# First-block attention: bias sum, negation and maximum in one VectorE instruction, the query's gate sum added by TensorE

## The chip, the cores and the metric

The kernel runs on one core of a Trainium2 chip. The metric is the device time of one launch in microseconds (us). A core has TensorE (PE in the profile; its weight loads are PEld), VectorE (DVE), ScalarE (ACT), GpSimd (POOL) and SyncE (SP, which here issues the weight loads from memory).

## The reference, cut to what matters

Two model blocks run one after the other. Only the attention of the first block is touched. It is run twice (DEPTH = 2 layers), each time with 8 heads of width 64 on 256 tokens, in query blocks of 128:

```python
cum = jnp.cumsum(log_f.astype(jnp.float32), axis=1).transpose(0, 2, 1)   # 8 x 256
...
logits = jnp.einsum("bhqd,bhkd->bhqk", qi, k).astype(jnp.float32) * scale
logits = logits + ci[..., :, None] - cum[:, :, None, :]
logits = jnp.where(kpos[None, :] <= qpos[:, None], logits, -jnp.inf)
p = jax.nn.softmax(logits, axis=-1)
return jnp.einsum("bhqk,bhkd->bhqd", p.astype(v.dtype), v)
```

So each logit is a product of query and key, plus the gate sum of the query (`ci`), minus the gate sum of the key, masked. The rest of the first block (a 31-tap convolution, a gated recurrence, an output projection, a large product-key layer) and the whole second block stay as they are.

## The kernel before, in words

Every engine has one program in a fixed order; semaphores order them against each other. Weights come as tiles of 128x1024 into a ring of four, are split by ACT into a high part `Wh` (L1207) and by DVE into a low part `Wl` (L1698), and PE multiplies both. A layer of the first block begins with 20 such tiles of input projection (16 tiles `m_` = 0..15 and 4 value tiles), then comes the attention, then the output projection.

Within the projection, PE also does small work between tiles. At `m_ == 12` it turns the gate sums `cum` (8 partitions x 256) into columns in bank 5, and DVE copies them to `cT` (L1890). In `gate_spread` PE spreads the negated key sums `ncum` over all 128 partitions with the selector `sel` (8x128 for a head), and DVE adds the mask in `gate_bias` and keeps the result in `biasT` (L1875 to L1877). The attention begins when the last `gate_bias` is done.

The attention is a software pipeline over `h` = 0..9. PE's turn `h` holds, in this order:

- the scores of head h+1 (`head_scores`): one fp32 matmul of 128 columns for the first query block, and one of 256 for the second, into bank 4 or 5. The operands lie on partitions 0 to 63 for an even head and 64 to 127 for an odd one;
- in turns 0 and 1, 4 and 5 filler matmuls (`keep_clock`, bf16, 512 columns, result unused);
- the product of probabilities and values of head h-2 (from the transposed `PT`);
- three transposes of the probabilities `Pm` of head h-1 (L749), which wait for DVE's `p_ready`;
- in turns 2 to 6, 3 filler matmuls.

DVE's turn `h` holds: two `scalar_tensor_tensor` for head h (scores + `cT` + `biasT`, 128 and 256 columns, L1927 and L1929), a wait for its own semaphore `att_sc`, two `tensor_reduce` for the negated maximum (L1933, L1934), then for head h-1 the reciprocal of the sums (L1939), two scalings of `Pm` (L1940, L1941, which signal `p_ready`), and two taps of the convolution (four instructions of L1856).

ACT's turn holds the two exponentials with their sums (L1319, L1321), the copy of the transposed probabilities (L1328), and now and then a copy of a finished head pair (L1333) and of a part of the mixer's output (L1310, in turn 6). The buffers of scores, `Pm` and `PT` are double.

After turn 9 come a layer norm and 18 filler matmuls, and the output projection.

Of the kernel before, what the change touches and what calls it, by code (L numbers as in the profile page):

```python
# [12 lines left out]
ALU = mybir.AluOpType  # L13
ACT = mybir.ActivationFunctionType
AXX = mybir.AxisListType.X


P = 128
D = 1024
C = D // P  # L20
T = 256
T2 = 2 * T
L = 2
HEADS, HD = 8, 64
# [249 lines left out]
def build(nc, wts, mod_d, cst_d, keys_d, mla_d, bias_d, x_d, ctx_d, out_d, stop_after=None):  # L274
    ctx = ExitStack()
    with ctx:
# [85 lines left out]
        PT = [arena[:, i * 3 * P:(i + 1) * 3 * P] for i in range(2)]  # L362
        cT = area(2, HEADS)

# [178 lines left out]
        def _(pe):  # L543
# [120 lines left out]
            def gate_spread(l, i):  # L664

                if i:
                    pe.wait_ge(S("bc_ev"), 5 * l + i)
                for h in (2 * i, 2 * i + 1):
                    m = mm(bank[6 - i % 2][:, (h % 2) * T:(h % 2 + 1) * T], sel[0:HEADS, h, :], ncum[0:HEADS, :], True, True)
                m.then_inc(S("bc_mm"), 1)  # L670
# [6 lines left out]
            for l in range(L):  # L677
# [4 lines left out]
                for m_ in range(16):  # L682
# [21 lines left out]
                    if m_ == 12:  # L704
                        pe.wait_ge(S("cum_ready"), l + 1)
                        pe.wait_ge(S("rg_ev"), 2 * l + 2)
                        for tt in range(2):
                            m = mm(bank[5][:, tt * HEADS:(tt + 1) * HEADS], cum[0:HEADS, tt * P:(tt + 1) * P],
                                   ident[0:HEADS, 0:HEADS], True, True)
                        m.then_inc(S("bc_mm"), 1)  # L710
                    if m_ in (13, 14):
# [6 lines left out]
                pe.wait_ge(S("proj_ev"), N_EV * (l + 1))  # L718
                pe.wait_ge(S("bc_ev"), 5 * (l + 1))
                def head_scores(h):  # L720
                    po, hc, b = slice(64 * (h % 2), 64 * (h % 2) + 64), h // 2, bank[4 + h % 2]
                    if h >= 2:
                        pe.wait_ge(S("att_sc"), HEADS * l + h - 1)
                    mm(b[:, 0:P], qT[po, hc, 0:P], kT[po, hc, 0:P], True, True)
                    mm(b[:, P:3 * P], qT[po, hc, P:T], kT[po, hc, :], True, True).then_inc(S("att_mm"), 1)

                head_scores(0)
                for h in range(HEADS + 2):
# [22 lines left out]
                    if 2 <= h < 7:  # L751
                        keep_clock(3, bank[3])
                    if h == HEADS:
# [425 lines left out]
        def _(act):  # L1179
# [67 lines left out]
            for l in range(L):  # L1247
# [64 lines left out]
                for h in range(HEADS + 2):  # L1312
                    if h < HEADS:
                        act.wait_ge(S("att_mx"), HEADS * l + h + 1)
                        if h >= 2:
                            act.wait_ge(S("pt_mm"), HEADS * l + h - 1)
                        nm = col[:, 8 + 2 * (h % 2):10 + 2 * (h % 2)]
                        sm = col[:, 12 + 2 * (h % 2):14 + 2 * (h % 2)]
                        nc.scalar.activation(Pm[h % 2][:, 0:P], sc[h % 2][:, 0:P], ACT.Exp, bias=nm[:, 0:1],  # L1319
                                             accum_out=sm[:, 0:1])  # L1320
                        nc.scalar.activation(Pm[h % 2][:, P:], sc[h % 2][:, P:], ACT.Exp, bias=nm[:, 1:2],  # L1321
                                             accum_out=sm[:, 1:2]).then_inc(S("att_exp"), 1)
# [324 lines left out]
        def _(dve):  # L1647
# [158 lines left out]
            for l in range(L):  # L1806
# [62 lines left out]
                def gate_bias(i):  # L1869

                    dve.wait_ge(S("bc_mm"), 5 * l + i + 2)
                    src = bank[6 - i % 2][:, :].rearrange("p (a b) -> p a b", a=2)
# [15 lines left out]
                seq(v.tensor_tensor(bx[:, :, :], ig[:, :, :], xr[:, :, :], ALU.mult))  # L1888
                dve.wait_ge(S("bc_mm"), 5 * l + 1)
                v.tensor_copy(cT[:, :, :], bank[5][:, 0:2 * HEADS].rearrange("p (a b) -> p a b", a=2)).then_inc(S("bc_ev"), 1)  # L1890
                taps(14, 16)
# [20 lines left out]
                gate_bias(3)  # L1912
                dve.wait_ge(S("bc_ev"), 5 * (l + 1))
                def mix_low(p):
# [6 lines left out]
                for h in range(HEADS + 1):  # L1921
                    if h < HEADS:
                        dve.wait_ge(S("att_mm"), HEADS * l + h + 1)
                        if h >= 2:
                            dve.wait_ge(S("att_exp"), HEADS * l + h - 1)
                        s_, b = sc[h % 2], bank[4 + h % 2]
                        v.scalar_tensor_tensor(out=s_[:, 0:P], in0=b[:, 0:P], scalar=cT[:, 0, h:h + 1],  # L1927
                                               in1=biasT[:, h, 0:P], op0=ALU.add, op1=ALU.add)
                        v.scalar_tensor_tensor(out=s_[:, P:], in0=b[:, P:3 * P], scalar=cT[:, 1, h:h + 1],  # L1929
                                               in1=biasT[:, h, P:], op0=ALU.add, op1=ALU.add).then_inc(S("att_sc"), 1)  # L1930
                        dve.wait_ge(S("att_sc"), HEADS * l + h + 1)
                        nm = col[:, 8 + 2 * (h % 2):10 + 2 * (h % 2)]
                        v.tensor_reduce(nm[:, 0:1], s_[:, 0:P], AXX, ALU.max, negate=True)  # L1933
                        v.tensor_reduce(nm[:, 1:2], s_[:, P:], AXX, ALU.max, negate=True).then_inc(S("att_mx"), 1)  # L1934
                    if h >= 1:
# [519 lines left out]
```

## Time and profile before

| | |
|---|---|
| median of 3 runs | 3141.77 us (3140.1 to 3142.35) |
| the profiled execution's own time | 3144.92 us |
| its span (first to last instruction) | 3143.0 us |
| PE busy, share of the span | 97% |
| DVE busy | 72% |
| ACT busy | 44% |
| mean granted TensorE clock | 0.992 |
| attention with its prologue and layer norm | about 40 us, twice (98 to 138 us and 1098 to 1138 us) |

The profile is of one execution; its own time lies 3.15 us above the median of the timed runs, and 1.9 us of it lie outside the span. Busy shares are means over stages that have different limits, so the attention is read from its own stretch. Times of single instructions are start and duration on one engine; an engine may begin an instruction before the record of the one ahead of it has ended, so the distance from one start to the next is what an instruction costs.

### The profile page before, as it was taken

Reading aid. Unit: us, or ns where it says so; the run is one execution under the profiler, and the core shown is the slowest. Engines: PE = TensorE matmul, PEld = TensorE weight load, DVE = VectorE, ACT = ScalarE, POOL = GpSimd, SP = SyncE. Lnnn points to the kernel's source line nnn. Section 1 sums busy time; section 2 is a strip of 40 time slices with the busy share of each in tenths; the row PEclk is TensorE's granted clock in tenths of the full one; section 3 lists DMA queues with packets and bytes.
Section 4 is the critical chain, followed back from the end, with each engine's and each line's share of the span. In section 5 each row is a group of like instructions: output and inputs, shape, how many; then the busy total and the mean of one; then the engine's idle time right before and its main releaser. Section 6 shows DMA issues by size and latency. Waiting matters only on the chain. (4 is left out here: it accounts for less than half of the span.)

```text
span 3143.0 us, 59178 instructions
## 1 busy us (share of the span) xinstructions
PE 3049.7 (97%) x22446; PEld 2667.8 (85%) x22446; DVE 2270.8 (72%) x3842; ACT 1377.4 (44%) x2167; POOL 248.0 (8%) x195
## 2 busy tenths in 40 slices
PE   8899999999999989999999999999999989998999
PEld 7699988989887769998998988776778878874999
DVE  7778877787887869887777798676456764665446
ACT  5445444443444544535344344445432223436444
POOL 0064000000000017100000000000001100001000
PEclk9999999999999999999999999999999999999999
DMA  4245565464555324646556456420035542321354
GB/s 166 87 141 196 167 208 192 164 246 151 168 187 190 131 72 162 209 160 233 170 189 216 156 167 220 137 98 8 15 116 191 201 161 94 107 88 61 128 182 155
DMA packets 131892, 478.44 MB, mean 152 GB/s; under 512 B 14593, under 2 KB 16641, under 8 KB 131329
## 3 DMA queue, kind: packets, MB, share of 16 engines
q1 hardware_dynamic: 115904, 416.72, 39.6%
q0 software_dynamic: 15808, 59.25, 5.7%
q8 instruction: 122, 2.00, 0.3%
q14 instruction: 58, 0.47, 0.1%
HBM read 474.87 MB, written 1.05 MB: 151 GB/s over the span
## 5 line engine op out<-in xcount | busy, mean ns | idle before, releaser
L1698 DVE TENSOR_TENSOR Wl<-ring,Wh 128x1024 fp32r<-128x1024 f32 x720 | 878.4, 1222 | 560.9 <-ACT Wh L1207 558.6
L545 PE MATMUL bank<-HR,Wh 128*128 128x256 f32 (+1 forms) x7488 | 1143.0, 303 | 6.6 <-DVE HR L1918 4.0
L1207 ACT CAST Wh<-ring 128x1024 fp32r<-128x1024 f32 x788 | 824.1, 1046 | 609.0 <-PE bank L545 609.0
L545 PEld LDWEIGHTS bank<-HR,Wh 128*128 128x128 f32 x7488 | 1011.8, 191 | 65.7 <-issue 14.1
L545 PE MATMUL bank<-HR,Wl 128*128 128x256 f32 (+1 forms) x3744 | 612.0, 300 | 10.1 <-DVE Wl L1698 10.1
L545 PE MATMUL bank<-Wh,HR 128*128 128x512 f32 x2304 | 577.2, 394 | 1.1 <-DVE HR L2105 0.8
L545 PEld LDWEIGHTS bank<-HR,Wl 128*128 128x128 f32 x3744 | 525.3, 191 | 33.9 <-DVE Wl L1698 11.5
L545 PEld LDWEIGHTS bank<-Wh,HR 128*128 128x128 f32 x2304 | 428.5, 188 | 96.0 <-issue 8.4
L545 PE MATMUL bank<-arena 128*128 128x32 f16 (+5 forms) x5128 | 305.1, 213 | 15.4 <-DVE arena L1877 6.2
L545 PE MATMUL bank<-Wl,HR 128*128 128x512 f32 x1152 | 306.1, 389 | 0.0
L1436 ACT ACTIVATE arena<-bank 128x256 f32 (+1 forms) x256 | 98.3, 384 | 470.5 <-PE bank L545 470.3
L545 PEld LDWEIGHTS bank<-arena 128*128 128x128 f16 (+3 forms) x5128 | 223.7, 112 | 84.7 <-issue 41.7
L545 PEld LDWEIGHTS bank<-Wl,HR 128*128 128x128 f32 x1152 | 216.3, 188 | 45.3
L2400 POOL TENSOR_TENSOR Wl<-ring,Wh 128x1024 fp32r<-128x1024 f32 x68 | 163.8, 2416 | 101.3 <-ACT Wh L1207 101.0
L2081 DVE TENSOR_TENSOR arena<-arena 128x2048 f16<-128x2048 f16 x128 | 155.8, 1218 | 0.1
L2409 POOL DMA_DIRECT2D HA<-mods x48 | 36.0, 749 | 1361.1 <-DVE arena L1672 1024.0
L545 PE MATMUL bank<-FR,Wh 128*128 128x512 f32 (+1 forms) x704 | 132.0, 340 | 8.1 <-DVE modv L1681 8.1
L545 PEld LDWEIGHTS bank<-FR,Wh 128*128 128x128 f32 x704 | 110.6, 192 | 23.0 <-DVE modv L1681 8.5
L1674 DVE SCALAR_TENSOR_TENSOR arena<-arena,csil 128x1024 f32<-128x1024 f32 x84 | 104.1, 1280 | 6.9 <-DMA arena<-mods 4.8
L2105 DVE TENSOR_TENSOR HR<-arena,HR 128x256 fp32r<-128x256 f32 x256 | 106.7, 420 | 1.1 <-ACT HR L1380 0.9
L1674 DVE SCALAR_TENSOR_TENSOR arena<-HA,csil,arena 128x1024 f32<-128x1024 f32 x84 | 107.1, 1316 | 0.0
L2089 DVE TENSOR_TENSOR arena<-arena 128x512 f16<-128x512 f16 x256 | 97.3, 421 | 12.2
(254 smaller groups left out, 2153.9 us busy)
## 6 DMA issues: line engine op xcount, KB each, us to landing
ring<-weights SPq DMA_DIRECT2D x788, 512.0 KB, 3.3
HA<-mods POOLq DMA_DIRECT2D x48, 512.0 KB, 4.0
arena<-mods POOLq DMA_DIRECT2D x48, 512.0 KB, 3.6
arena<-bias POOLq DMA_DIRECT2D x16, 256.0 KB, 3.2
arena<-keys POOLq DMA_DIRECT2D x2, 1024.0 KB, 5.3
arena<-mla POOLq DMA_DIRECT2D x1, 1536.0 KB, 6.4
X<-x SPq DMA_DIRECT2D x1, 1024.0 KB, 6.6
X<-context POOLq DMA_DIRECT2D x1, 1024.0 KB, 7.1
```

The costliest lines, as they stand in the source:

```text
L545: return nc.tensor.matmul(out, lhsT, rhs, start=first, stop=last)
L1207: nc.scalar.copy(Wh[:, i % SPL], ring[:, i % RAW]).then_inc(S("hi_done"), 1)
L1436: nc.scalar.activation(o, bank[s % 2][:, 0:T], ACT.Gelu_apprx_tanh).then_inc(S("h_ev"), 1)
L1674: m = v.scalar_tensor_tensor(out=out[:, j], in0=w, scalar=by, in1=out[:, j], op0=ALU.mult, op1=ALU.add)
L1698: v.tensor_tensor(Wl[:, i % SPL], ring[:, i % RAW], Wh[:, i % SPL], ALU.subtract).then_inc(S("lo_done"), 1)
L2081: v.tensor_tensor(Aoh[s % 2], pairs(if12h[:, 0, at]).broadcast_to([P, BT // 2, P, 2]), iotar.unsqueeze(1).broadcast_to([P, BT // 2, P, 2]) ...
L2089: m = v.tensor_tensor(Bg[s % 2][:, part], Boh[s % 2], pairs(gpart[:, part, at]).broadcast_to([P, BT // 2, EQ, 2]), ALU.mult)
L2105: v.tensor_tensor(Hl[:, s % MV, 0:T], GH[q % 2][:, bass.ds(it * R + s, 1), :] .rearrange("p o t -> p (o t)"), Hh[:, s % MV, 0:T], ALU.subt ...
L2400: nc.gpsimd.tensor_tensor(Wl[:, i % SPL], ring[:, i % RAW], Wh[:, i % SPL], ALU.subtract)\
L2409: pool.dma_start(mod_slot(n), mod_d[n].rearrange("p (a b) -> p a b", a=4)).then_inc(S(f"mod_in{n % 2}"), 16)
```

## The change

Four edits, all for the attention of the first block.

- The query's gate sum is no longer turned into `cT` and added by DVE. PE adds it in the scores' bank, with a matmul of `cum` (8 partitions x 128, the stationary operand) and the head's selector (8x128), once for each 128 columns: three more fp32 matmuls for a head. The step at `m_ == 12`, DVE's copy and one semaphore count go.
- DVE's four instructions for a head become two `tensor_tensor_reduce`: each writes -(scores + `biasT`) and its minimum, which is the negated maximum of the logits.
- ACT's exponentials take scale -1.0.
- PE's filler matmuls in turns 2 to 6 go from 3 to 1, and the scores of head h+1 wait for `att_mx` instead of `att_sc`.

```diff
@@ gate_spread
-                if i:
-                    pe.wait_ge(S("bc_ev"), 5 * l + i)
+                if i >= 2:
+                    pe.wait_ge(S("bc_ev"), 4 * l + i - 1)
@@ PE, m_ == 12
                         pe.wait_ge(S("rg_ev"), 2 * l + 2)
-                        for tt in range(2):
-                            m = mm(bank[5][:, tt * HEADS:(tt + 1) * HEADS], cum[0:HEADS, tt * P:(tt + 1) * P],
-                                   ident[0:HEADS, 0:HEADS], True, True)
-                        m.then_inc(S("bc_mm"), 1)
@@ PE, head_scores
                     if h >= 2:
-                        pe.wait_ge(S("att_sc"), HEADS * l + h - 1)
-                    mm(b[:, 0:P], qT[po, hc, 0:P], kT[po, hc, 0:P], True, True)
-                    mm(b[:, P:3 * P], qT[po, hc, P:T], kT[po, hc, :], True, True).then_inc(S("att_mm"), 1)
+                        pe.wait_ge(S("att_mx"), HEADS * l + h - 1)
+                    mm(b[:, 0:P], qT[po, hc, 0:P], kT[po, hc, 0:P], True, False)
+                    mm(b[:, 0:P], cum[0:HEADS, 0:P], sel[0:HEADS, h, :], False, True)
+                    mm(b[:, P:3 * P], qT[po, hc, P:T], kT[po, hc, :], True, False)
+                    for a in range(2):
+                        m = mm(b[:, (1 + a) * P:(2 + a) * P], cum[0:HEADS, P:T], sel[0:HEADS, h, :], False, a == 1)
+                    m.then_inc(S("att_mm"), 1)
@@ PE, turns 2 to 6
-                        keep_clock(3, bank[3])
+                        keep_clock(1, bank[3])
@@ ACT
-                        nc.scalar.activation(Pm[h % 2][:, 0:P], sc[h % 2][:, 0:P], ACT.Exp, bias=nm[:, 0:1],
+                        nc.scalar.activation(Pm[h % 2][:, 0:P], sc[h % 2][:, 0:P], ACT.Exp, bias=nm[:, 0:1], scale=-1.0,
@@ DVE, projection
-                dve.wait_ge(S("bc_mm"), 5 * l + 1)
-                v.tensor_copy(cT[:, :, :], bank[5][:, 0:2 * HEADS].rearrange("p (a b) -> p a b", a=2)).then_inc(S("bc_ev"), 1)
@@ DVE, attention
-                        v.scalar_tensor_tensor(out=s_[:, 0:P], in0=b[:, 0:P], scalar=cT[:, 0, h:h + 1],
-                                               in1=biasT[:, h, 0:P], op0=ALU.add, op1=ALU.add)
-                        v.scalar_tensor_tensor(out=s_[:, P:], in0=b[:, P:3 * P], scalar=cT[:, 1, h:h + 1],
-                                               in1=biasT[:, h, P:], op0=ALU.add, op1=ALU.add).then_inc(S("att_sc"), 1)
-                        dve.wait_ge(S("att_sc"), HEADS * l + h + 1)
                         nm = col[:, 8 + 2 * (h % 2):10 + 2 * (h % 2)]
-                        v.tensor_reduce(nm[:, 0:1], s_[:, 0:P], AXX, ALU.max, negate=True)
-                        v.tensor_reduce(nm[:, 1:2], s_[:, P:], AXX, ALU.max, negate=True).then_inc(S("att_mx"), 1)
+                        v.tensor_tensor_reduce(s_[:, 0:P], b[:, 0:P], biasT[:, h, 0:P], -1.0, 3.0e38, ALU.add, ALU.min, nm[:, 0:1])
+                        v.tensor_tensor_reduce(s_[:, P:], b[:, P:3 * P], biasT[:, h, P:], -1.0, 3.0e38, ALU.add, ALU.min,
+                                               nm[:, 1:2]).then_inc(S("att_mx"), 1)
```

## Rows read from the trace of the kernel before

**Rows 1.** The page, part 1: busy us of each engine, share, instructions.

```profile
PE 3049.7 (97%) x22446; PEld 2667.8 (85%) x22446; DVE 2270.8 (72%) x3842; ACT 1377.4 (44%) x2167; POOL 248.0 (8%) x195
```

**Rows 2.** Windows, attention's turns: length, PE, PEld, DVE, ACT, POOL busy, clock, DMA.

```profile
103.50:125.00 21.50, 15.76 (x79) 8.78 (x80) 21.08 (x67) 10.13 (x35) 0.00 (x0) 1.00 0.00 1
```

**Rows 3.** Timeline, one turn of the pipeline: start, us, engine, line, instruction, idle before.

```profile
108.53 0.34 DVE L1927 SCALAR_TENSOR_TENSOR arena<-bank,arena 128x128 f32<-128x128 f32 x1
108.79 0.47 DVE L1929 SCALAR_TENSOR_TENSOR arena<-bank,arena 128x256 f32<-128x256 f32 x1
...
109.83 0.15 DVE L1939 RECIPROCAL col<-col 128x2 f32<-128x2 f32 x1
...
110.62 0.55 PE L749 MATMUL bank<-K,arena 128*128 128x128 f32 x3 [0.70 <-DVE arena L1941]
...
112.07 0.34 DVE L1927 SCALAR_TENSOR_TENSOR arena<-bank,arena 128x128 f32<-128x128 f32 x1
```

**Rows 4.** Timeline of PE, the same turn, narrow windows (rows*columns of the array).

```profile
107.08 0.55 PE L749 MATMUL bank<-K,arena 128*128 128x128 f32 x3 [1.35 <-DVE arena L1941]
107.47 0.81 PE L545 MATMUL bank<-K 128*128 128x512 bf16 x3
107.90 0.38 PE L545 MATMUL bank<-K 128*128 128x512 bf16 x1
108.21 0.37 PE L545 MATMUL bank<-arena 64*128 64x128 f32 x1
108.42 0.49 PE L545 MATMUL bank<-arena 64*128 64x128 f32 x2
108.75 0.38 PE L545 MATMUL bank<-arena 64*128 64x256 f32 x1
109.06 0.43 PE L545 MATMUL bank<-arena 128*64 128x256 f32 x1
```

**Rows 5.** Timeline of PE, a key spread (8 rows) and the value tile behind it.

```profile
87.08 0.48 PE L545 MATMUL bank<-arena 8*128 8x256 f32 x1
87.40 0.38 PE L545 MATMUL bank<-arena 8*128 8x256 f32 x1
...
88.13 0.50 PE L545 MATMUL bank<-Wh,HR 128*128 128x512 f32 x1
```

**Rows 6.** Timeline of PE, the attention's start: scores of heads 0 and 1, fillers, first transposes.

```profile
99.15 0.39 PE L545 MATMUL bank<-arena 64*128 64x128 f32 x2 [3.12 <-DVE arena L1877]
...
100.01 1.04 PE L545 MATMUL bank<-K 128*128 128x512 bf16 x4
...
103.54 0.55 PE L749 MATMUL bank<-K,arena 128*128 128x128 f32 x3 [0.46 <-DVE arena L1941]
```

**Rows 7.** Timeline of DVE, two tensor_tensor_reduce in a row in the second block.

```profile
2842.80 0.69 DVE L2332 CUSTOM_DVE_ANT_0 arena<-bank,arena 128x512 f32<-128x512 f32 x1 [0.17 <-PE bank L545]
...
2843.42 0.69 DVE L2332 CUSTOM_DVE_ANT_0 arena<-bank,arena 128x512 f32<-128x512 f32 x1
```

**Rows 8.** Timeline, the last turns: transposes of heads 5 and 7, ACT's work between them.

```profile
121.23 0.55 PE L749 MATMUL bank<-K,arena 128*128 128x128 f32 x3 [0.70 <-DVE arena L1941]
...
121.82 0.48 ACT L1328 COPY arena<-bank 128x384 f32<-128x384 f32 x1 [0.28 <-PE bank L749]
122.19 0.62 ACT L1310 CAST HR<-arena 128x512 fp32r<-128x512 f32 x1
...
124.09 0.40 ACT L1319 ACTIVATE arena<-arena,col 128x128 f32<-128x128 f32 x1 [1.28 <-DVE col L1934]
...
124.89 0.19 ACT L1321 ACTIVATION_READ_ACCUMULATOR arena<-arena,col 128x1 f32 x1
...
127.05 0.55 PE L749 MATMUL bank<-K,arena 128*128 128x128 f32 x3 [0.30 <-DVE arena L1941]
```

**Rows 9.** Timeline of PE, the step at `m_ == 12` and the tile behind it.

```profile
69.77 0.61 PE L545 MATMUL bank<-K,arena 8*128 8x8 f32 x4
...
70.31 2.18 PE L545 MATMUL bank<-HR,Wh 128*128 128x256 f32 x16
```

More of the change, by code:

```diff
@@ L362, in build @@
         PT = [arena[:, i * 3 * P:(i + 1) * 3 * P] for i in range(2)]
-        cT = area(2, HEADS)
         top[0] = 16384
@@ L718, in _ @@
                 pe.wait_ge(S("proj_ev"), N_EV * (l + 1))
-                pe.wait_ge(S("bc_ev"), 5 * (l + 1))
+                pe.wait_ge(S("bc_ev"), 4 * (l + 1))
                 def head_scores(h):
@@ L1318, in _ @@
                         sm = col[:, 12 + 2 * (h % 2):14 + 2 * (h % 2)]
-                        nc.scalar.activation(Pm[h % 2][:, 0:P], sc[h % 2][:, 0:P], ACT.Exp, bias=nm[:, 0:1],
+                        nc.scalar.activation(Pm[h % 2][:, 0:P], sc[h % 2][:, 0:P], ACT.Exp, bias=nm[:, 0:1], scale=-1.0,
                                              accum_out=sm[:, 0:1])
-                        nc.scalar.activation(Pm[h % 2][:, P:], sc[h % 2][:, P:], ACT.Exp, bias=nm[:, 1:2],
+                        nc.scalar.activation(Pm[h % 2][:, P:], sc[h % 2][:, P:], ACT.Exp, bias=nm[:, 1:2], scale=-1.0,
                                              accum_out=sm[:, 1:2]).then_inc(S("att_exp"), 1)
@@ L1869, in gate_bias @@
                 def gate_bias(i):
-                    dve.wait_ge(S("bc_mm"), 5 * l + i + 2)
+                    dve.wait_ge(S("bc_mm"), 4 * l + i + 1)
                     src = bank[6 - i % 2][:, :].rearrange("p (a b) -> p a b", a=2)
@@ L1912, in _ @@
                 gate_bias(3)
-                dve.wait_ge(S("bc_ev"), 5 * (l + 1))
+                dve.wait_ge(S("bc_ev"), 4 * (l + 1))
                 def mix_low(p):
```

## The prediction

> **What bounds the kernel now.** I read the page first. PE is busy 97% of the span [rows 1], but that is a mean over stages, so it says nothing yet of the attention. The windows of the attention's turns say more: of 21.5 us DVE is busy 21.08, PE 15.76, ACT 10.13, and no weights move [rows 2]. DVE sets the pace there. The timeline shows how. From one L1927 to the next is 3.54 us (108.53 to 112.07), with no idle time on DVE, and PE's transposes wait 0.70 us for DVE's L1941 [rows 3]. So in a turn PE has some slack, but not much, and the change takes work from DVE and gives work to PE. The question is which of the two is longer afterwards.
>
> **What PE's passes cost.** An fp32 matmul is two records. In the score part the first pass of 128 columns starts at 108.21, the second at 108.42, the third (256 columns) 0.11 later and the fourth at 108.75; before them the last filler starts at 107.90 and the fillers are 0.22 apart (107.47 to 107.90 is two of them) [rows 4]. So a pass of 128 columns takes 0.11, one of 256 takes 0.22, a filler 0.22. Two places don't fit. The filler at 107.90 is through at 108.11, but the scores start at 108.21; and the second pass comes 0.21 behind the first and not 0.11. That is 0.09 plus 0.10 lost where the array goes from 128 rows to 64. The same two losses stand where it goes from 64*128 to 128*64 (108.75 + 0.22 = 108.97, next start 109.06), and from 128 rows to 8 and back: the first 8-row pass has 0.32 to the second, where 0.22 is the stream, and from 87.40 three passes of 0.22 end at 88.05, while the next tile starts at 88.13 [rows 5]. I take 0.19 for a change of the array's shape into an fp32 matmul.
>
> **DVE, part by part.** Removed are the four instructions from 108.53 to 109.83, 1.30 us a head, a wait on DVE's own semaphore included [rows 3]. Added are two `tensor_tensor_reduce`. The second block has this instruction at 512 columns, 0.61 from start to start with its accumulator read hidden [rows 7]. 0.53 of it is the stream at one column in 1.04 ns (its cost over 128-column and 256-column neighbours of the same kind grows like that: L1927 and L1929 differ by 0.13 in duration for 128 columns), the rest is fixed, 0.08. So 0.21 and 0.35, together 0.56. DVE's turn would be 3.54 - 1.30 + 0.56 = 2.80 us. Even at the 0.61 of the 512-column form twice it would be 3.46. ACT's exponentials with scale -1 cost what they did. If DVE alone counted, seven turns would give 5 us a layer.
>
> **PE, part by part.** A turn now: transposes to fillers 0.39 (107.08 to 107.47), three fillers and the change to 64 rows 0.74, scores 0.85 (108.21 to 109.06), values 0.70 (0.27, 0.22, 0.11, 0.11) and 0.09 to the next transposes; sum 2.77 against 3.54, a slack of 0.77 [rows 4]. The change takes two fillers out, -0.43. It adds three fp32 matmuls of 128 columns, six passes, 0.65. And it alternates 64-row and 8-row matmuls: 64, 8, 64, 8, 8, then the values. That is three more changes of shape in each head. No row shows a change between 64 and 8 rows. From below it costs nothing (heads 0 and 1, on different halves of the rows, start together at 99.15 and lose nothing [rows 6]); from above I put the gap plus a full pass of latency, 0.09 + 0.27, as if each change waited for the record's end. Nearest are the changes above, all 0.19, whichever two shapes meet, so I take 0.19, three times 0.57. PE's turn becomes 2.77 - 0.43 + 0.65 + 0.57 = 3.56. PE then sets the pace, at what DVE had: the turn gains nothing.
>
> The Trainium skill, in TensorEngine Tiling (Array Packing), section Key Properties, says that changing the tiling mode, not just the tile, drains TensorE. The page speaks against this change, since 64 and 8 rows are two modes; by it the sum is mine, and without it the sum is that of the first rival.
>
> **The start.** Today the scores of heads 0 and 1 run together, 99.15 to 100.01, 0.86 [rows 6]. With 8-row matmuls between they can't: a head's scores are 0.85 + 0.65 + 0.57 = 2.07, two are 4.1, so the fillers start 3.2 later. Head 2's scores are another 1.2 longer. The first transposes, which today wait 0.46 for DVE at 103.54 [rows 6], came then at 99.15 + 4.11 (two heads) + 0.97 (4 fillers, change) + 2.07 (head 2) + 1.09 (5 fillers) = 107.4, which is 3.9 late. DVE's part of that (first maximum, exponential, reciprocal, scaling) is done before 105. From there to the transposes of head 5 are five turns, the first without filler and so 0.2 shorter: 17.6 instead of 17.7. They start 3.7 later than 121.23.
>
> **The end.** The last two turns have no scores. Today 5.82 us pass from the transposes of head 5 to those of head 7 (121.23 to 127.05), because DVE is late [rows 8]. After the change DVE is ahead and the chain is ACT's: copy and mixer copy done 1.6 after the transposes (121.23 to 122.81), head 7's exponentials 1.0 (124.09 to 125.08), copy of head 6 about 0.45, values 0.8: 3.8. That gives back 2.0. So a layer's attention ends 3.7 - 2.0 = 1.7 later.
>
> **The projection.** The four 8x8 passes go: 69.77 to 70.31, 0.54 [rows 9]. PE has no other wait there, the low part for the next tile is ready only about 0.1 before it would be needed, and the attention's start follows PE through the last value tile. I take 0.5 a layer; from below nothing. DVE's copy of 0.17 is hidden beside PE.
>
> **Sum.** (1.7 - 0.5) x 2 = +2.4 us. Span 3143.0 becomes 3145.4, with 1.9 outside it 3147.3 for a profiled execution; the median stood 3.15 lower than the profiled one, so 3144.2. What follows the attention (layer norm, 18 fillers, output projection) only moves. The clock was 1.00 in the turns [rows 2]; PE is now busier there, so two fillers less shouldn't lower it.
>
> A change under 0.2%, 6.3 us, can't be told from none here.
>
> **Rivals.**
>
> *Changes between 64 and 8 rows are free.* For it: heads 0 and 1 lose nothing between two 64-row halves. Against: those have one shape, and every change of shape in the rows costs. Then PE's turn is 2.99, still over DVE's 2.80; the first transposes come 2.2 late, head 5's 0.8 early, the end 2.8 early, with the projection 3.3 a layer: 6.6, time 3135.2, just past the bound. If only the 0.09 is lost each time it lies halfway to the forecast, near 3140.
>
> *Odd heads overlap.* Odd heads lie on rows 64 to 127, the 8-row operands on rows 0 to 7, and two matmuls on different rows did run together [rows 6]. Then, changes being free too, an odd head's scores stay at 0.85 and PE averages 2.7 a turn, just under DVE's 2.80: head 5's transposes come 3.4 early, the end 5.4, with the projection 5.9 a layer, time 3130. Against: the shapes differ, and both write one bank.
> The Trainium skill's page TensorE: Matmul & The Clock Gate, Part 3, says that matmuls on different row groups overlap; the trace agrees for two 64-row ones (starts both at 99.15), and by that rule the time would be this rival's.
>
> *A change from 64 to 8 rows costs more than the others* and the kernel is slower. Its place is the same three changes, since both sides add into one bank, one on top of the other's sum. At 0.36 each a head's scores are 0.5 longer, eight of them before head 5's transposes make 4.1 us a layer: 3152. It decides from 0.27 a change on: the bound is 3.15 a layer, 1.2 are in the sum, and 1.95 over 24 changes is 0.08 more than 0.19.
>
> *DVE's instruction doesn't get cheaper.* If it took twice its stream, DVE's turn would be 3.3, still under PE's 3.56: no effect on the time.
>
> **How the numbers follow.** The forecast (PE's turn about as long as DVE's was) 0.60, its own range 3141 to 3147.5 (0.05 either way in each of nine turns). Changes free 0.11, half of them 0.10, overlap 0.08, dearer changes 0.10, other 0.01. Faster by over 0.2%: the overlap 0.08, most of the free case 0.08, a little of the rest 0.02, together 0.18. Slower: the dearer case 0.10 and 0.01. Within: 0.71. The predicted time is 3144.2. The range reaches from just past the free case, 3134, to 3149, leaving out the overlap and most of the dearer case.
>
> **What would show it.** In the trace after: the 128-column scores followed by an 8-row pass 0.2 later than the stream; a head's scores 2.07 from first to last; transposes 3.5 to 3.6 apart and no longer released by DVE but following PE; DVE idle 0.7 a turn; `tensor_tensor_reduce` 0.21 and 0.35 apart; transposes of head 0 near 107, of head 7 near 128. A turn of 3.0 says the changes are free, one of 2.8 released by DVE that they overlap, one over 3.8 that they are dear.

## The result and the profile after

The changed kernel takes 3159.28 us (median of 4 runs, 3155.96 to 3167.41), beside 3142.06 for the kernel before (4 runs, 3140.1 to 3143.82): a ratio of 1.0057, interval 1.0045 to 1.0068, some 17 us slower. The forecast was 3144.2 with a range to 3149. The profiled execution took 3157.23 us, with a span of 3155.4 and a mean granted clock of 0.988. The other three runs show how much hangs on that last number: 3155.96 at 0.988, 3161.34 at 0.987, 3167.41 at 0.985. The two profiled executions are only 12.3 us apart (3144.92 and 3157.23), the medians 17.2. What is taken from the traces below explains the 12; the other 5 lie in the choice of the profiled runs, and no trace shows where.

Part 1 of the page of the changed kernel answers to [rows 1]:

```profile
PE 3074.2 (97%) x22514; PEld 2683.2 (85%) x22514; DVE 2260.7 (72%) x3840; ACT 1377.1 (44%) x2167; POOL 248.3 (8%) x195
```

PE has 68 records more and 24.5 us more of busy time. At full clock the change would be 14 of these: 16 heads by 1.22 (0.65 of passes and 0.57 of changes), less 20 fillers of 0.22 and two steps of 0.54. So the other matmuls must have become longer somewhere. The page doesn't say where: its clock line, in 40 slices, is 9 everywhere. Windows do. Of the changed kernel: the low stretch of layer 0's attention and the rest of its turns, then 40 us around each attention, then the low stretch of layer 1 (each row: length, busy times of PE, PEld, DVE, ACT and POOL, clock, DMA share, GB/s):

```profile
99.60:113.30 13.70, 13.70 (x39) 7.60 (x38) 6.34 (x26) 2.58 (x10) 0.00 (x0) 0.50 0.00 1
113.30:130.10 16.80, 16.80 (x86) 10.53 (x85) 12.11 (x49) 6.74 (x26) 0.00 (x0) 1.00 0.01 1
95.00:135.00 40.00, 36.11 (x150) 21.79 (x150) 23.44 (x87) 14.28 (x46) 0.00 (x0) 0.83 0.05 16
1095.00:1135.00 40.00, 36.88 (x142) 22.16 (x140) 22.44 (x78) 12.93 (x37) 0.00 (x0) 0.79 0.14 48
1103.10:1120.20 17.10, 16.39 (x44) 9.41 (x44) 6.91 (x28) 2.38 (x10) 0.00 (x0) 0.50 0.10 31
```

The same windows of the kernel before:

```profile
95.00:135.00 40.00, 29.15 (x145) 15.64 (x145) 32.07 (x92) 21.05 (x55) 0.00 (x0) 1.00 0.06 25
1095.00:1135.00 40.00, 29.14 (x145) 15.63 (x145) 32.07 (x92) 21.04 (x55) 0.00 (x0) 1.00 0.07 25
```

The clock column is the result. Before, it was 1.00 in both attentions (2.4 GHz); now it is 0.50 (1.2 GHz) for 13.7 us in the first and 17.1 us in the second, and 1.00 again from 113.3 and 1120.2 on. Look at PE's busy time in the low stretch of layer 0: 13.70 of 13.70. Nothing is idle there; the engine is full of work and slow. The two falls don't come at the same place: in layer 0 at 99.6, within the first scores, in layer 1 at 1103.1, in the 3.12 us of idle time and 0.7 before the first scores.

Timeline of PE in the changed kernel, layer 0, to be laid beside [rows 4, 6]:

```profile
97.97 6.25 PE L544 MATMUL bank<-arena 64*128 64x128 f32 x20 [3.12 <-DVE arena L1876]
104.15 1.89 PE L544 MATMUL bank<-K 128*128 128x512 bf16 x4
105.97 3.81 PE L544 MATMUL bank<-arena 64*128 64x128 f32 x10
109.71 2.31 PE L544 MATMUL bank<-K 128*128 128x512 bf16 x5
111.81 0.85 PE L748 MATMUL bank<-K,arena 128*128 128x128 f32 x3
...
119.35 0.55 PE L748 MATMUL bank<-K,arena 128*128 128x128 f32 x3
119.73 0.38 PE L544 MATMUL bank<-K 128*128 128x512 bf16 x1
120.04 2.96 PE L544 MATMUL bank<-arena 64*128 64x128 f32 x14
122.93 0.55 PE L748 MATMUL bank<-K,arena 128*128 128x128 f32 x3
...
133.91 0.55 PE L748 MATMUL bank<-K,arena 128*128 128x128 f32 x3
```

The ten passes of head 2's scores take 3.81 at 1.2 GHz, and two heads 6.18 (97.97 to 104.15), the first 1.6 of it at full clock. Once the clock is back, the turn is regular: 119.35 to 122.93 is 3.58. The transposes at the front of the turn have no release in brackets any more: they follow PE itself. DVE waits instead. Timeline of PE and DVE in one such turn, narrow windows, beside [rows 3, 4]:

```profile
116.46 0.49 PE L544 MATMUL bank<-arena 64*128 64x128 f32 x2
116.88 0.37 PE L544 MATMUL bank<-arena 8*128 8x128 f32 x1
117.29 0.48 PE L544 MATMUL bank<-arena 64*128 64x256 f32 x1
117.91 0.37 PE L544 MATMUL bank<-arena 8*128 8x128 f32 x1
118.55 0.43 PE L544 MATMUL bank<-arena 128*64 128x256 f32 x1
```

```profile
118.66 0.29 DVE L1925 CUSTOM_DVE_ANT_0 arena<-bank,arena 128x128 f32<-128x128 f32 x1 [0.69 <-PE bank L544]
118.87 0.42 DVE L1926 CUSTOM_DVE_ANT_0 arena<-bank,arena 128x256 f32<-128x256 f32 x1
119.22 0.16 DVE L1932 RECIPROCAL col<-col 128x2 f32<-128x2 f32 x1
```

These are the scores of head 4, an even one. They take 2.09 (116.46 to 118.55). The next turn, with head 5, is as long (119.35 to 122.93). DVE's two instructions are 0.21 and 0.35 apart, and it stands idle 0.69 for PE in every turn.

**Where the time went.** From the first scores to the last transposes of layer 0 it is now 35.94 us (97.97 to 133.91), where it was 27.90 [rows 6, 8]: 8.0 longer. A turn is 3.58 at full clock and 6.47 at half clock (a_fill_idle, below), so each microsecond at half clock loses 1 - 3.58/6.47 = 0.447; 13.7 lose 6.1. The rest, 1.9, is what the forecast had as 1.7. The same two ends in layer 1:

```profile
1103.81 7.51 PE L544 MATMUL bank<-arena 64*128 64x128 f32 x20 [3.12 <-DVE arena L1876]
...
1140.92 0.55 PE L748 MATMUL bank<-K,arena 128*128 128x128 f32 x3
```

That is 37.11, 9.2 longer. Of the low stretch 16.4 us lie behind the first scores; they lose 16.4 x 0.447 = 7.3, and the rest is 1.9 again. The start of layer 0's attention came 1.18 earlier, half of it from the step taken out at `m_ == 12`; the other half was there before the first tile of the projection, so the change has no part in it. So the clock costs 6.1 + 7.3 = 13.4 us in the two attentions, and the instructions of the change 1.9 + 1.9, less 0.6 twice for the projection, 2.6: together 16.0. The span grew by 12.4. The difference of 3.6 is the lead of 0.6 and 3.0 from behind the attentions. The kernel before had 3.4 us at 0.50 there, as its windows show, and the changed one has none: the same stretch of the output projection on PE takes 8.93 before (138.39 to 147.32) and 7.42 after (145.26 to 152.68), 1.5 less in each layer. That the low stretch of before isn't there any more is luck: no edit aims at it.

```profile
138.40:141.80 3.40, 3.40 (x16) 3.40 (x17) 0.00 (x0) 0.44 (x1) 0.69 (x1) 0.50 0.37 77
1138.50:1141.90 3.40, 3.40 (x17) 3.40 (x18) 0.00 (x0) 0.63 (x1) 0.55 (x1) 0.50 0.52 159
```

### The profile page after: what moved, and what is told of

The parts are those of the page before. It is cut to its first block and busy times, and to the rows that moved or that the text cites. A ratio compares the mean times of both kernels' runs of the same rounds, so it can differ in the third digit from the quotient of the medians.

```text
span 3155.4 us, 59312 instructions
## 1 busy us (share of the span) xinstructions
PE 3074.2 (97%) x22514; PEld 2683.2 (85%) x22514; DVE 2260.7 (72%) x3840; ACT 1377.1 (44%) x2167; POOL 248.3 (8%) x195
## 5 line engine op out<-in xcount | busy, mean ns | idle before, releaser
L544 PE MATMUL bank<-arena 128*128 128x32 f16 (+8 forms) x5224 | 335.5, 217 | 16.1 <-DVE arena L1876 6.2
L544 PEld LDWEIGHTS bank<-arena 128*128 128x128 f16 (+4 forms) x5224 | 244.4, 115 | 95.9 <-issue 50.4
L2393 POOL TENSOR_TENSOR Wl<-ring,Wh 128x1024 fp32r<-128x1024 f32 x68 | 163.9, 2418 | 98.2 <-ACT Wh L1206 97.9
```

The lines of the kernel that those rows point to most:

```text
L544: return nc.tensor.matmul(out, lhsT, rhs, start=first, stop=last)
L2393: nc.gpsimd.tensor_tensor(Wl[:, i % SPL], ring[:, i % RAW], Wh[:, i % SPL], ALU.subtract)\
```

## The experiments

The question left by the profile: what makes the clock fall, and what keeps it down? The matmuls on few rows themselves (64 and 8, changing shape at each), the 3.12 us of idle time ahead of them, or the fillers taken out? Each kernel below was timed beside the kernel before on the same chip. "Half clock" is the time at 0.50 in the two attentions of the profiled execution, in us. One execution is profiled, and which one differs: it is the slowest of its runs in c, e, g and i, the fastest in b and m. Nor does all of the spread come from the attentions: from one and the same matmul behind both layers of the first block (at 2147.35 in the kernel before) to the end, code that no edit touches, the profiled executions take between 991 us (c) and 1002 us (e and g), and 996 in the kernels before and after.

| kernel | edit | median us (range, runs) | ratio to before (interval) | half clock, layers 0 and 1 |
|---|---|---|---|---|
| a_fill_idle | after, idle time ahead filled | 3172.58 (3162.91–3174.31, 4) | 1.0085 (1.0064–1.0105) | 34.1, 34.1 |
| b_group | after, 8-row matmuls in one group | 3170.54 (3151.57–3183.82, 4) | 1.0102 (1.0071–1.0134) | 10.2, 13.7 |
| c_no_gate_k3 | DVE's half alone | 3128.82 (3125.71–3135.57, 4) | 0.9952 (0.9935–0.9969) | 13.7, 13.7 |
| d_pe_part | PE's half alone | 3165.54 (3160.59–3178.86, 4) | 1.0084 (1.0055–1.0112) | 41.0, 13.7 |
| e_before_k1 | before with 1 filler a turn | 3145.1 (3142.86–3153.11, 10) | 1.0005 (0.9995–1.0014) | 13.6, 6.8 |
| f_after_k3_fill | after, 3 fillers, idle filled | 3162.32 (3158.09–3166.78, 4) | 1.0061 (1.0043–1.0078) | 0, 30.7 |
| g_no_gate_fill | DVE's half, idle filled | 3128.19 (3126.35–3138.37, 5) | 0.9948 (0.9935–0.9962) | 3.4, 0 |
| h_rows64 | after, gate matmuls on 64 rows, even heads | 3148.53 (3144.36–3169.48, 10) | 1.0027 (1.0012–1.0042) | 10.2, 10.2 |
| k_fillers_inside | fillers in place of the gate matmuls | 3146.7 (3142.91–3157.47, 10) | 1.0014 (1.0001–1.0026) | 6.8, 6.8 |
| l_rows128 | after, gate matmuls on 128 rows | 3151.22 (3148.81–3162.12, 7) | 1.0026 (1.0007–1.0045) | 6.8, 13.7 |
| i_no_gate_k1 | DVE's half, 1 filler a turn | 3131.52 (3129.34–3141.54, 6) | 0.9961 (0.9948–0.9973) | 0, 37.5 |
| m_after_again | the changed kernel again | 3170.66 (3152.72–3179.55, 7) | 1.0082 (1.0055–1.0109) | 13.7, 17.1 |

### Is it the idle time ahead? (a_fill_idle)

```diff
-                keep_clock(4, bank[2])
+                keep_clock(18, bank[2])
                 pe.wait_ge(S("proj_ev"), N_EV * (l + 1))
```

> The changed kernel, with 18 filler matmuls instead of 4 ahead of the attention, so that PE has almost none of the 3.12 us of idle time before the first scores. Theory A (the clock falls because this idle time is followed by scores that load the array little): the granted clock stays 1.00 from 98 to 113 us, and the time is that of the forecast for the rest, 3142 to 3147. Rival B (the scores with their 8-row passes are by themselves too little, whatever stands before): the clock still falls within the scores of heads 0 to 2, a little later, and the time stays near 3156 to 3160.

Slower still, 3172.58, beyond both expectations. Timeline of PE, and a window:

```profile
97.14 1.03 PE L544 MATMUL bank<-K 128*128 128x512 bf16 x4
98.27 4.22 PE L544 MATMUL bank<-arena 64*128 64x128 f32 x20
102.43 1.46 PE L544 MATMUL bank<-K 128*128 128x512 bf16 x4
...
115.65 0.90 PE L748 MATMUL bank<-K,arena 128*128 128x128 f32 x3
...
122.12 0.90 PE L748 MATMUL bank<-K,arena 128*128 128x128 f32 x3
```

```profile
103.00:137.00 34.00, 34.00 (x95) 19.34 (x92) 16.64 (x64) 7.71 (x29) 0.00 (x0) 0.50 0.00 1
```

There is no idle time ahead of the scores now. They run at full clock for 4.1 us, as the sum had it for two heads, and then the clock falls all the same, at 102.9, and stays down for 34.1 us while PE is busy for all of them: a turn is 6.47 (115.65 to 122.12). Layer 1 has the same, from 1116.7 on, 4.7 behind its first scores. So idle time right ahead isn't needed for the fall.

### The order of the passes (b_group)

```diff
-                    mm(b[:, 0:P], cum[0:HEADS, 0:P], sel[0:HEADS, h, :], False, True)
-                    mm(b[:, P:3 * P], qT[po, hc, P:T], kT[po, hc, :], True, False)
-                    for a in range(2):
+                    mm(b[:, P:3 * P], qT[po, hc, P:T], kT[po, hc, :], False, False)
+                    for a in range(3):
...
```

Both score matmuls come first, then the three 8-row ones; two changes of shape fewer in each head.

> The changed kernel with a head's five matmuls in another order: both 64-row ones, then the three 8-row ones, so one change of the array's shape inside a head and not three. If a change costs the 0.20 that the trace after shows, a head's scores are 0.40 shorter, the turn is 3.18 instead of 3.58, the last transposes come 3 to 4 us earlier in each layer: 6 to 8 us less than the changed kernel, if the clock falls as it does there. Theory of the clock: it still falls near the first scores, so the time lies at 3149 to 3153. Rival (the changes of shape are what makes the clock fall): it stays 1.00 and the time is below 3140.

Timeline of PE, two sets of transposes:

```profile
116.68 0.55 PE L747 MATMUL bank<-K,arena 128*128 128x128 f32 x3
...
119.88 0.55 PE L747 MATMUL bank<-K,arena 128*128 128x128 f32 x3
```

3.20 a turn in place of 3.58: two changes fewer are 0.38, so 0.19 each. That settles the price of a change, on which the rivals differed. The new order did not make the kernel faster, against the expectation of 3149 to 3153: the four runs spread from 3151.57 to 3183.82, with clocks from 0.987 down to 0.977, and the trace is of the fastest.

### DVE's half alone (c_no_gate_k3, g_no_gate_fill, i_no_gate_k1)

A number that is the same for all keys of a query falls out of the softmax. So the query's gate sum can simply be left out of the logits: no `cT` and no 8-row matmul. In c:

```diff
-                    mm(b[:, 0:P], qT[po, hc, 0:P], kT[po, hc, 0:P], True, False)
-                    mm(b[:, 0:P], cum[0:HEADS, 0:P], sel[0:HEADS, h, :], False, True)
-                    mm(b[:, P:3 * P], qT[po, hc, P:T], kT[po, hc, :], True, False)
-                    for a in range(2):
-                        m = mm(b[:, (1 + a) * P:(2 + a) * P], cum[0:HEADS, P:T], sel[0:HEADS, h, :], False, a == 1)
-                    m.then_inc(S("att_mm"), 1)
+                    mm(b[:, 0:P], qT[po, hc, 0:P], kT[po, hc, 0:P], True, True)
+                    mm(b[:, P:3 * P], qT[po, hc, P:T], kT[po, hc, :], True, True).then_inc(S("att_mm"), 1)
@@ turns 2 to 6
-                        keep_clock(1, bank[3])
+                        keep_clock(3, bank[3])
```

g has the 18 fillers of a_fill_idle on top; i is c with one filler a turn.

> DVE's part alone: the tensor_tensor_reduce stay, the three 8-row matmuls are left out and the fillers are 3 again, as before. The query's gate sum is added to every logit of a row, which softmax takes out again, so what is computed is the same. Theory (DVE's part is worth what its turn says, the loss is all PE's): two heads' scores run together again, the clock stays 1.00, the turn is 2.85 (PE 2.77 plus a gap; DVE 2.80), the attention ends about 5 us earlier in each layer, and with 0.5 a layer from the projection the time is 3130 to 3133. Rival (tensor_tensor_reduce or the finished fillers take part in the loss): slower than before.

> DVE's part alone (no 8-row matmuls, 3 fillers a turn, as in the run of DVE's part) plus 18 fillers ahead of the attention in PE's idle time. Theory (the fall at 97.9 us in the profile of DVE's part came from the 3.12 us of idle time ahead): the clock stays 1.00 through the attention in every run, 3124 to 3128, and the spread shrinks to 3 us. Rival (the idle time has no part in it): as DVE's part alone, 3126 to 3136.

> DVE's part alone (no gate matmuls), but with 1 filler a turn as in the change. At full clock DVE's 2.80 sets the turn, PE's work is 2.34 of it: 3126 to 3129 if the clock holds. If the fillers are what brings the clock back after the start (the run of the filler cut alone took 10 to 13 us less clock only at times): some executions several us slower, median 3128 to 3136.

All three beat the kernel before, by 0.4 to 0.5%, and so the changed one too. Timeline of PE in g:

```profile
105.23 0.55 PE L744 MATMUL bank<-K,arena 128*128 128x128 f32 x3 [0.44 <-DVE arena L1930]
108.03 0.55 PE L744 MATMUL bank<-K,arena 128*128 128x128 f32 x3
110.83 0.55 PE L744 MATMUL bank<-K,arena 128*128 128x128 f32 x3
```

A turn is 2.80, and the distance from the first scores to the last transposes 22.61 (98.89 to 121.50), 5.3 less than before. c came out 1 us under the range expected. Its profiled run is the slowest of its four, 3135.57; the clock fell at 97.9 in the idle time, before the first scores at 98.68, and was down for 13.7 us. So a fall can come in idle time too. In g, with that time filled, the attentions were at half clock for 3.4 us and not at all, yet the median is the same within its range and the spread no smaller, where 3 us had been expected. g's profiled run is its slowest, 3138.37, and not for its attentions: its second block takes 11 us longer than c's. i shows the two levels side by side, layer 0 and layer 1:

```profile
98.00:122.00 24.00, 19.49 (x101) 11.09 (x102) 20.92 (x84) 12.81 (x44) 0.00 (x0) 1.00 0.07 23
1092.00:1125.00 33.00, 32.29 (x91) 16.20 (x87) 21.12 (x83) 11.83 (x43) 0.00 (x0) 0.50 0.02 8
```

The same program has turns of 2.80 in one and 4.31 in the other, where the clock is down for 37.5 us. No 8-row matmul is in it, so the gate matmuls are not the only thing that can keep the clock down; i has one filler a turn, as the changed kernel has.

### PE's half alone (d_pe_part)

The scores, gate matmuls and single filler of the changed kernel; on DVE the four instructions of before, with the constant 0.0 in the place of `cT`, and ACT without the scale of -1.

```diff
+                        v.scalar_tensor_tensor(out=s_[:, 0:P], in0=b[:, 0:P], scalar=0.0,
+                                               in1=biasT[:, h, 0:P], op0=ALU.add, op1=ALU.add)
...
-                        v.tensor_tensor_reduce(s_[:, 0:P], b[:, 0:P], biasT[:, h, 0:P], -1.0, 3.0e38, ALU.add, ALU.min, nm[:, 0:1])
...
+                        v.tensor_reduce(nm[:, 0:1], s_[:, 0:P], AXX, ALU.max, negate=True)
...
```

> PE's part alone: the three 8-row matmuls and one filler a turn stay, DVE has its four instructions of before (the two sums with a constant 0 in the place of cT, since the query's sum is in the bank). Theory (PE sets the pace after the change and loses the clock at the start): within 2 us of the changed kernel, 3156 to 3161, clock 0.50 for 13 us or more in each attention. Rival (DVE's custom instruction is what costs): near the kernel before, 3140 to 3146.

3165.54, a loss at least as large as that of the whole change (over 4 us above the range expected). The clock was down for 41.0 us in layer 0 (turn 6.47) and 13.7 in layer 1 (turn 3.58 after it). PE's half (gate matmuls and fillers taken out) carries all of the loss.

### The fillers (e_before_k1, f_after_k3_fill)

```diff
@@ e: the kernel before
-                        keep_clock(3, bank[3])
+                        keep_clock(1, bank[3])
@@ f: the changed kernel
-                keep_clock(4, bank[2])
+                keep_clock(18, bank[2])
...
-                        keep_clock(1, bank[3])
+                        keep_clock(3, bank[3])
```

> The kernel before, with the filler cut alone: 1 filler instead of 3 in turns 2 to 6, nothing else. DVE sets the turn of 3.54 us there and PE's work falls from 2.77 to 2.34. Theory F (the fillers hold the clock, since the attention's own matmuls use few rows and columns): the clock falls in some attentions and stays low through the turns; PE's turn at 1.2 GHz is about 4.3 us, so up to 5 us an attention, time 3145 to 3152 with a wider spread. Rival (the filler cut is harmless, the loss needs the 8-row passes): 3140 to 3145, clock as before.

> The changed kernel with 3 fillers a turn as before, and 18 fillers ahead of the attention. Theory F: the clock may still fall in the scores of heads 0 to 2, but comes back soon after, so the turns run at 4.01 us (3.58 + 0.43) at full clock; time 3150 to 3158, the spread narrower than that of the changed kernel with 18 fillers ahead alone (3163 to 3174). Rival (fillers do nothing for the clock against 8-row passes): still 0.50 through the turns, 3170 or more.

Two fillers less alone cost the kernel before nothing that can be told in time (1.0005). But the clock was down in e's attentions, for 13.6 and 6.8 us, where the profile of the kernel before has none. Window of e, layer 0, and timeline of its PE:

```profile
95.00:135.00 40.00, 30.14 (x126) 16.07 (x125) 30.88 (x92) 19.65 (x53) 0.00 (x0) 0.83 0.05 16
```

```profile
98.34 1.11 PE L545 MATMUL bank<-arena 64*128 64x128 f32 x8 [3.12 <-DVE arena L1877]
...
127.05 0.90 PE L749 MATMUL bank<-K,arena 128*128 128x128 f32 x3
```

From the first scores to the last transposes it is 28.71 (98.34 to 127.05), only 0.8 more than the 27.90 of before, though 11 us of it ran at half clock. DVE sets the pace there, and PE, which waits 1.13 for it in a turn at full clock, has slack to be slow in. At the 0.447 of the changed kernel the 11 us would have cost 4.9. So the change did two things: it brought more half clock, and it made each microsecond of it dear, because PE has no slack left.

Two fillers more don't save the changed kernel: 3162.32, between the two ranges expected. Windows of f, layer 0 and layer 1:

```profile
98.00:129.60 31.60, 30.95 (x154) 18.76 (x154) 21.22 (x83) 11.95 (x43) 0.00 (x0) 1.00 0.05 17
1103.70:1134.40 30.70, 30.70 (x85) 16.70 (x84) 14.25 (x55) 6.69 (x25) 0.00 (x0) 0.50 0.00 1
```

One program, one execution, the same instructions: in layer 0 the clock never fell, in layer 1 it was down for 30.7 us. Layer 0 is also the one attention with 8-row passes that is at full clock from end to end:

```profile
98.08 4.22 PE L544 MATMUL bank<-arena 64*128 64x128 f32 x20
...
129.57 0.55 PE L748 MATMUL bank<-K,arena 128*128 128x128 f32 x3
```

It takes 31.49. Two extra fillers lengthen the four turns in which PE sets the pace, from 3.58 to 4.01; in turn 6 they fall into a wait for ACT. Less 4 x 0.43 that is 29.8, against 27.90: +1.9, the same as the rest left by the clock's part in both layers of the changed kernel, where the forecast had +1.7.

### Rows or changes of shape? (h_rows64, k_fillers_inside, l_rows128, m_after_again)

h runs the even heads' gate matmuls on 64 rows, those above 8 filled with zeros, so that those heads have one shape throughout; the odd heads keep 8 rows. l does it on 128 rows for all heads, k leaves the gate sum out and has a 128-row filler in the place of the first gate matmul and two in the place of the others.

```diff
@@ h
+                    gr = HEADS if h % 2 else 64
...
-                    mm(b[:, 0:P], cum[0:HEADS, 0:P], sel[0:HEADS, h, :], False, True)
+                    mm(b[:, 0:P], cum[0:gr, 0:P], sel[0:gr, h, :], False, True)
...
@@ l
+                    mm(b[:, 0:P], cum[0:P, 0:P], sel[0:P, h, :], False, True)
...
@@ k
+                    mm(b[:, 0:P], qT[po, hc, 0:P], kT[po, hc, 0:P], True, True)
+                    keep_clock(1, bank[3])
+                    mm(b[:, P:3 * P], qT[po, hc, P:T], kT[po, hc, :], True, True).then_inc(S("att_mm"), 1)
+                    keep_clock(2, bank[3])
```

> The changed kernel with the gate-sum matmuls of even heads on 64 rows (cum and the selector with zeros in rows 8 to 63, set by two more DVE instructions a layer), those of odd heads as they are. Theory (the 0.20 between 64-row and 8-row passes is the change of the array's shape): an even head's scores take 1.50 us instead of 2.09, from the stream alone, an odd head's stay at 2.09; turns alternate between 3.0 and 3.58 at full clock. Rival (the 0.20 is the price of adding onto a sum in the same bank): both 2.09. The clock: if rows in use are what counts, the attention of this kernel loses it less often than the changed kernel, median 3145 to 3155; if not, about 3155.

> The changed kernel with the three 8-row gate matmuls of a head left out and fillers in their places (128 rows, bf16, 512 columns, result unused): one between the two score matmuls, two behind them. What is computed is the same, since softmax takes the query's sum out. The array changes its shape as often as in the changed kernel and PE's scores take nearly as long (about 1.9 instead of 2.09 us), so PE is as busy; only what it does there has all rows. Theory G (the clock goes by how much of the array works, and 8 of 128 rows hardly count): the clock comes back at once after the idle time, the time is 3136 to 3142, with a spread like that of the kernel before. Rival H (the many changes of shape, in which PE stands still though it is shown busy, let the clock fall): half clock for 10 us or more in each attention, 3150 to 3160.

> The changed kernel with the gate matmuls of all heads on 128 rows, rows 8 to 127 of both operands zero (two more DVE instructions a layer). Stream time and changes of shape as in the changed kernel, turn 3.58 at full clock. Theory G, if rows that hold zeros count as rows: full clock soon after the start, 3143 to 3150. Theory G, if zeros don't count, and rival H: as the changed kernel, 3156 to 3165.

> The changed kernel itself once more, on the same chip as the three beside it. 3155 to 3168 as before; half clock in both attentions of the profile, over a stretch that differs between them, and a turn of 3.58 wherever the clock is full.

k, l and m ran beside each other. k and l keep all changes of shape. Timeline of PE, a turn of l and one of k:

```profile
119.82 0.55 PE L748 MATMUL bank<-K,arena 128*128 128x128 f32 x3
...
123.42 0.55 PE L748 MATMUL bank<-K,arena 128*128 128x128 f32 x3
```

```profile
117.89 0.55 PE L746 MATMUL bank<-K,arena 128*128 128x128 f32 x3
...
121.28 0.55 PE L746 MATMUL bank<-K,arena 128*128 128x128 f32 x3
```

l's turns are 3.59 in the mean (this one 3.60, the one ahead of it 3.58), k's 3.39. At 8 rows (m) the median is 3170.66, at 128 rows with zeros (l) 3151.22, with fillers (k) 3146.7. The last two are 1 and 5 us above the ranges expected. The median of the mean clocks is 0.983 for m and 0.990 for l and k. So 19 us go when the same matmuls at the same length run on more rows, zeros though they hold, and the number of changes alone is not what keeps the clock down. In the profiled executions, of which m's is the fastest of seven, the difference is smaller: 30.8 us at half clock in m, 20.5 in l, 13.6 in k. The size is less sure than the sign: the first four runs of the changed kernel had a ratio of 1.0057, the seven here 1.0082, against l's 1.0026 (1.0007 to 1.0045). In h, timeline of PE:

```profile
116.68 0.55 PE L749 MATMUL bank<-K,arena 128*128 128x128 f32 x3
...
120.26 0.55 PE L749 MATMUL bank<-K,arena 128*128 128x128 f32 x3
120.65 0.38 PE L544 MATMUL bank<-K 128*128 128x512 bf16 x1
120.95 2.38 PE L544 MATMUL bank<-arena 64*128 64x128 f32 x14
123.27 0.55 PE L749 MATMUL bank<-K,arena 128*128 128x128 f32 x3
```

The turn with an odd head's scores is 3.58, the one with an even head's 3.01 (120.26 to 123.27), the scores 1.52 in place of 2.09: three changes of shape less are 0.57. That is the forecast's term a third time.

m is the changed kernel over again. Its median is above the 3155 to 3168 expected. Its seven runs lie from 3152.72 at a clock of 0.989 to 3179.55 at 0.980, so time follows the mean clock with some 2.9 us for each 0.001. Worked out from the turns, 0.001 of the mean is 0.002 x 3150 = 6.3 us at half clock, which lose 6.3 x 0.447 = 2.8. The spread of the changed kernel is the spread of the length of its low stretches. Where in the program the longer ones of the slow runs lie isn't shown, since the trace is of the fastest; 27 us is more than the 11 by which the second block differs between the traces.

## Why the prediction was wrong

**The step that failed** is in the part on the sum: "The clock was 1.00 in the turns [rows 2]; PE is now busier there, so two fillers less shouldn't lower it." Busy time was taken for what holds the clock. In the profile after, PE is busy 13.70 of 13.70 us at 0.50, in a_fill_idle 34.00 of 34.00. What takes that step's place: with the short 64- and 8-row passes that now fill the attention, the clock falls to 1.2 GHz, for 13.7 and 17.1 us in the changed kernel and for 10 to 41 us in all but one attention of its relatives with 8-row passes (a, b, d, f, h), and each of these microseconds loses 0.45, because PE now sets the pace. The traces show that most of the loss comes by the clock, d that it comes with PE's half, and l beside m that the rows have a part in it. It isn't shown that the 8-row passes alone make the clock fall: c, e and i have none, and their clock fell too, for up to 13.7, 6.8 and 37.5 us at a stretch. None of the rivals had this; the dearer case had the sign, but by another mechanism that the turn of 3.58 rules out. Of the fillers taken alone the conclusion on the time stands, e_before_k1 is within 0.2%; that on the clock doesn't, 13.6 and 6.8 us at half clock in e's attentions.

**The terms of the sum held.**

- Change of shape 0.19: 0.20 in the trace (116.46 to 116.88 and 116.88 to 117.29 are 0.42 and 0.41 for two passes of 0.11), 0.19 from b_group, 0.19 from h_rows64. It is the same from 64 to 8 rows. The rivals that had it free or halved, or odd heads overlapping, fall: no score pass overlaps another in the turn of head 4 above, and the turn with head 5 is 3.58 too. The Trainium skill, TensorEngine Tiling (Array Packing), section Key Properties, has the change of mode draining the engine; the trace agrees, 0.20 a change.
- A head's scores 2.07: measured 2.09. PE's turn 3.56: 3.58. Fillers and transposes as they were.
- DVE's instruction 0.21 and 0.35: measured the same. DVE's turn 2.80: seen as the pace of i's layer 0, where PE waits for DVE in each turn. In the changed kernel it is 0.69 idle, forecast 0.7.
- The end: transposes of head 5 to those of head 7 are 3.83 (130.08 to 133.91), forecast 3.8.
- Attention 1.7 longer a layer: 1.9 in both layers with the clock's part taken off, 1.9 in f's layer 0 with its extra fillers taken off.
- Projection 0.5 a layer: 0.6 of the 1.18 by which layer 0 starts earlier.
- "What follows the attention only moves" did not hold, by luck of the clock: 1.5 a layer came back there, with the 3.4 us at half clock that the kernel before had.

By the forecast's own terms alone the sum is +2.6 us, forecast +2.4. The first transposes were to be at 107.4 and came at 111.81; here the clock was first visible.

**What stays open.** What sets off a fall and how long the low stretch lasts in an execution isn't settled: f has none and 30.7 us in two layers with the same instructions, and the changed kernel differs by 27 us from run to run. Idle time (c) and passes on few rows without any idle time right ahead (a) can each come before a fall; their shares in the changed kernel, which has both, were not told apart. Nor was the part of the fillers taken out: with three a turn the changed kernel still lost 30.7 us to half clock in one layer (f), and with one a turn DVE's half lost 37.5 without any gate matmul (i). Whether the odd heads gain like the even ones wasn't tried: their rows are the other half of the array, and both would add into one bank.

## What to carry to other kernels

A busy PE isn't a fast PE. Ahead of a change that puts matmuls on few rows into a stage, read that stage's granted clock, and price it at both levels: here instructions worth 1.9 us a layer came with a loss of 6 to 7 us to half clock. Half clock is dear where PE sets the pace (0.45 us for each) and cheap where it has slack (0.8 us for an attention in e). And before moving a term to another engine, ask whether the result needs it: the query's gate sum falls out of the softmax, and DVE's half without it is 14 us faster (3128.2 to 3128.8) than the kernel before.

## What the runs showed of the hardware that was not expected

- The clock stayed at 0.50 for 34.1 us while PE was busy for all of them, with fp32 passes on 64 and 8 rows, transposes and a filler a turn (a_fill_idle).
- Zeros on the idle rows helped: the same matmuls on 128 rows instead of 8, at the same turn (3.59 and 3.58), are 19 us less in the median beside each other (l, m), 8 us less against the changed kernel's first runs (3159.28). On 64 rows beside 64-row scores each of them also saves its change of shape, 0.19.
- At half clock the turn isn't twice as long: 6.47 against 3.58. A turn whose pace is DVE's at full clock, 2.80, becomes one of PE, 4.31 (i).
